# Two small tiles move from behind a kernel's weight tiles to ahead of them, which shifts these by 64 bytes

## The reference

```
h = rms_norm(x, norm_mix_pre);  z = h @ w_in              # 1024 x 2816
a = window_attention(rope(aq), rope(ak), av, sink);  r = retention(rq, rk, rv, rg, ...)
x = x + rms_norm(concat(a, r) @ w_out, norm_mix_post)
q = rms_norm(x) @ xa_wq;  kv = rms_norm(mem) @ xa_wkv     # cross-attention, 256 memory tokens
x = x + rms_norm(softmax(q k / 16) v @ xa_wo, norm_xa_post)
gate, up = split(rms_norm(x) @ ffn_w_gu);  f = (silu(gate) * up) @ ffn_w_down   # width 2816
x = x + rms_norm(f, norm_ffn_post)
```

## Time and profile before

| | |
|---|---|
| median of 3 runs | 1411.92 us (1411.61 to 1412.18) |
| span of the profiled execution, and its own time | 1411.1 us, 1411.1 us |
| TensorE (PE) busy | 1393.6 us, 6756 matmuls |
| weight loads (PEld) busy | 1154.0 us |
| VectorE, ScalarE, GpSimd busy | 858.8, 646.7, 822.7 us |
| DMA | 172.04 MB, mean 122 GB/s |
| granted TensorE clock | 1.000 |

### The profile page before, as it was taken

One profiled execution on the slowest core, in us unless ns is written; L12 is line 12 of the kernel. 1 busy time (PEld: TensorE's weight loads), 2 busy tenths in 40 slices (PEclk: granted clock), 3 DMA queues, 4 the chain that ended last, 5 costly groups with the idle time before them and its releaser, 6 DMA issues.

```text
span 1411.1 us, 18901 instructions
## 1 busy us (share of the span) xinstructions
PE 1393.6 (99%) x6756; PEld 1154.0 (82%) x6756; DVE 858.8 (61%) x1264; ACT 646.7 (46%) x1315; POOL 822.7 (58%) x574
## 2 busy tenths in 40 slices
PE   8999999999999999999999999999999999999998
PEld 7988888767988888888888888888888888878886
DVE  5699997887855767855267633333323333474868
ACT  6432233676544754354365433333333333544454
POOL 1597256103582665511354687777777774799653
PEclk9999999999999999999999999999999999999999
DMA  5676133100043464310535133333333324933353
GB/s 201 206 248 208 46 90 104 61 1 2 1 155 119 133 227 128 97 38 27 183 105 209 51 104 107 112 112 101 109 104 98 112 83 161 357 112 99 109 206 150
DMA packets 127309, 172.04 MB, mean 122 GB/s; under 512 B 9584, under 2 KB 73456, under 8 KB 127216
## 3 DMA queue, kind: packets, MB, share of 16 engines
q1 hardware_dynamic: 123776, 161.52, 34.5%
q10 hardware_dynamic: 3440, 9.32, 1.9%
HBM read 129.64 MB, written 41.16 MB: 121 GB/s over the span
## 4 chain that ended last, share of the span: by engine, by line
PE 84%; DVE 5%; POOL 4%; ACT 2%; issue 2%; DMA 2%; SPq 0%; DVEq 0%; POOLq 0%; ACTq 0%
PE ps L1167 24%; PE ps L1169 24%; PE ps L1168 24%; PE ps L1163 5%; PE ps L1598 2%; PE ps L1341 1%; PE ps L1455 1%; POOL wd L1133 1%; PE ps L1379 1%; DMA gain_b<-f_rows 1%; PE ps L1433 1%; POOL right_b L1124 1%; DVE x L3360 1%; POOL right_a L1124 1%; POOL ws L1081 1%
## 5 line engine op out<-in xcount | busy, mean ns | idle before, releaser
L1167 PE MATMUL ps<-w_hi,t_hi 128*128 128x512 f32 (+2 forms) x592 | 228.3, 386 | 1.7 <-DVE t_lo L2616 1.3
L1169 PE MATMUL ps<-w_hi,t_lo 128*128 128x512 f32 (+2 forms) x592 | 226.0, 382 | 0.0
L1168 PE MATMUL ps<-w_lo,t_hi 128*128 128x512 f32 (+2 forms) x592 | 224.4, 379 | 0.0
L962 POOL TENSOR_TENSOR w_lo<-raw,w_hi 128x512 fp32r<-128x512 f32 (+1 forms) x52 | 83.5, 1611 | 97.2 <-ACT w_hi L1877 97.0
L1167 PEld LDWEIGHTS ps<-w_hi,t_hi 128*128 128x128 f32 x592 | 112.0, 189 | 20.5 <-DVE t_lo L2616 1.9
L1169 PEld LDWEIGHTS ps<-w_hi,t_lo 128*128 128x128 f32 x592 | 111.8, 189 | 20.2
L1168 PEld LDWEIGHTS ps<-w_lo,t_hi 128*128 128x128 f32 x592 | 112.0, 189 | 19.2
L1051 POOL TENSOR_TENSOR w_lo<-raw,w_hi 128x512 fp32r<-128x512 f32 x32 | 41.9, 1316 | 99.1 <-ACT w_hi L2264 99.1
L3253 DVE TENSOR_TENSOR ev<-ps,ev 128x512 f32<-128x512 f32 x21 | 14.5, 692 | 138.6 <-PE ps L1169 138.6
L1877 ACT ACTIVATE w_hi<-raw 128x512 fp32r<-128x512 f32 (+1 forms) x52 | 31.5, 616 | 97.5 <-PE ps L1169 97.1
L2463 ACT ACTIVATE ev<-ps 128x512 f32<-128x512 f32 x63 | 37.7, 598 | 83.7 <-PE ps L1169 83.7
(11 more groups left out here) (374 smaller groups left out, 4042.3 us busy)
## 6 DMA issues: line engine op xcount, KB each, us to landing
raw_a<-in_ffn_w_gu_dram SPq DMA_DIRECT2D x44, 256.0 KB, 3.2
raw_b<-in_ffn_w_gu_dram SPq DMA_DIRECT2D x44, 256.0 KB, 3.2
f_rows<-fs SPq DMA_DIRECT2D x44, 256.0 KB, 3.7
gain_b<-f_rows SPq DMA_DIRECT2D x39, 256.0 KB, 2.8
tables<-f_rows SPq DMA_DIRECT2D x38, 256.0 KB, 2.6
f_rows<-fa SPq DMA_DIRECT2D x33, 256.0 KB, 3.4
raw<-in_xa_wkv_dram SPq DMA_DIRECT2D x32, 256.0 KB, 3.4
raw<-in_xa_wo_dram SPq DMA_DIRECT2D x32, 256.0 KB, 2.6
```

The costliest lines, as they stand in the source:

```text
L962: nc.gpsimd.tensor_tensor(w_lo[:, k, 0:width], raw[:, k, 0:width], w_hi[:, k, 0:width].bitcast(F32), ALU.subtract).then_inc(w_split, 1)
L1167: nc.tensor.matmul(out, a_hi, b_hi, start=start, stop=False, skip_group_check=onto)
L1168: nc.tensor.matmul(out, a_hi, b_lo, start=False, stop=False, skip_group_check=onto)
L1169: return nc.tensor.matmul(out, a_lo, b_hi, start=False, stop=stop, skip_group_check=onto)
```

## The change

`zero` and `eps`, tiles of one float32 for each partition, 32 bytes each with the rounding, are allocated right behind `ident` and ahead of region R; before, they stood behind `gain_b`. R, `tables`, `gain_a` and `gain_b` thereby start 64 bytes further on. `ident`, `one` and everything behind it keep their places. No instruction, semaphore or transfer is added, removed or moved.

```diff
         ident = sb("ident", [P, P])
+        zero = sb("zero", [P, 1])
+        eps = sb("eps", [P, 1])
 
         R = overlay(
...
         gain_a = sb("gain_a", [P, D])
         gain_b = sb("gain_b", [P, D])
-        zero = sb("zero", [P, 1])
-        eps = sb("eps", [P, 1])
         one = sb("one", [P, 1])
```

## The result

The changed kernel takes 1416.48 us (median of 6 runs, 1415.59 to 1417.14) beside 1412.17 us of the kernel before (6 runs, 1411.61 to 1412.55): a ratio of 1.0031, 95% interval 1.0019 to 1.0042. It is slower by 4.3 us. The forecast was 1414.2 us, in a range of 1401.5 to 1420.

The account below looks back on a forecast made before the run. TensorE's matmul spacing was taken to bound the kernel. Moving from R +3.2, 416-wide +0.4, stationary in R -1.3, switches and other engines 0, sum +2.3 us on 1411.9: 1414.2 us, range 1401.5 to 1420.

Parts of the forecast that it names:

- The bound and the place: TensorE, busy 1393.6 of 1411.1 us, bounds the kernel; the change can act only through the spacing of its matmul starts.
- d, the distance modulo 256: Moving tile's offset less the stationary tile's, modulo 256, sets matmul spacing: 226.7 ns at 0, 228.8 at 64, 233.3 at 192.
- I take the value on the line through 0, 64 and 192: Matmul spacing at the new, unmeasured distance of 128 bytes, claimed to be 231.1 ns by a straight line.
- Moving from R: 1464 512-wide matmuls with moving tile in R, stationary in H or Z: 228.9 to 231.1 ns, +3.2 us.
- Stationary in R: 588 matmuls of query projection, its sums and FFN with `wz`: 233.4 to 231.1 ns, -1.3 us.
- 416-wide: 192 matmuls 416 columns wide, each slowed by 2.2 ns: +0.4 us.
- Switches between R and Z: Slow settling after some 21 pairs of switches in the down projection: 0 us, bound -1.1 us.
- B: Rival: period 128 bytes, or 128 as good as 0, so all regions agree; 1403.3 us, -0.6%; chance 0.25.
- C: Rival: both kinds of matmul, moving or stationary in R, go to 228.9 ns; 1409.3 us; chance 0.09.
- E: Rival: no effect, spacing follows something else and the port rule holds for small shifts; 1411.9 us; chance 0.08.
- D: Rival: distance 128 conflicts as badly as 192; 1419.4 us, up to 1434.2 at the outer bound; chance 0.15.
- A: The forecast case: spacing at 128 lies in between, 230.1 to 232.0 ns; 1414.2 us, own range 1412 to 1416.3; chance 0.38.

## Why the prediction came out as it did

**The bound and the place: right.** (Of the 17 us in which PE isn't busy the prediction showed 5; another 5.4 lie behind the last matmul, which starts at 1405.28. That doesn't touch the argument.) PE set the end, no wait came or went, and the change acted through the spacing alone. That the other tiles' 64 bytes cost nothing was assumed, and the run with `tables` and the gains alone showed it (1412.31).

**d, the distance modulo 256: right.** It was read out of four stretches of one trace. The period (R 256 bytes on: 1412.5) and the independence of the place (everything 64 bytes on: 1412.49; H and Z in R's stead: 1404.32 beside 1404.12) came out. The independence of the role came out at 0, 32, 64, 192 and 224 bytes, within 0.1 ns between the input and the query projection; at 128 there are 232.4 and 233.3 ns, and as both also occur in one role, d fixes the spacing there to 1 ns and no better.

**"I take the value on the line through 0, 64 and 192": wrong.** This is the step that failed. The one-to-three ratio of 2.2 and 6.7 ns is an accident. Measured are 226.7 at 0, 228.9 at 64 and 232.4 to 234.3 at all six other multiples of 32. There is a floor at 0, a lesser one at 64, and a plateau. The line gave 231.1 ns at 128 for both kinds; it is 232.4 to 233.3 where the moving tile lies in R and 233.3, no less than before, where the stationary one does. The prediction had said that if one group changed and the other didn't, d wasn't the one cause. That sign came (+3.5 and 0.0 ns in the stretches named) and misled: it presumed that a change of d always changes the spacing, and 128 and 192 lie on one plateau.

**The terms.** Moving from R: +3.2 us forecast, +4.3 measured by the table of stages (the 96 with `z_r` belong to the input projection, not to the output one; their number stands). Stationary in R (query projection and FFN up): -1.3 forecast, +0.1 measured. 416-wide: +0.4 forecast, -0.3 measured. Their 2.3 ns over 186.7 at d = 64 were read rightly, but they are no excess over d = 0: with R 192 bytes on the same 20 intervals take 3.77 us again, 188.5 ns. This width has another curve (3.74 us at 128 and 192, 3.85 at 32, 3.86 at 96), lower at 128 and 192, where the 512-wide ones are slower. Switches between R and Z: 0 forecast, -0.3 measured over the whole down projection, and the reason was wrong. Two steps of 128 bytes were to cost as much as one of 64 and one of 192; but a pair of 24 and 24 takes 10.93 us with 64 and 192, 10.90 with 128 and 10.88 with 0. The errors, +1.1, +1.4, -0.7 and -0.3, make 1.5 of the 2.3 us between 1414.2 and 1416.5. Of the rest 0.3 us is the base (1411.9 beside 1412.2), and 0.5 is the difference between the medians and this pair of traces. So the total came near in part by errors that cancelled.

**The rivals.** B (a period of 128) and C (228.9 ns for both kinds) are out. E is out: 8 us hang on 64 bytes. By the rule weighed there (the Trainium skill, "SBUF — State Buffer", section "Who interferes with whom": PE has a read port for each operand and waits for no one), as the prediction worked it out, none of these kernels should differ from another. The measurements, 1404.1 to 1420.2 us, decide against taking it as a promise that the operands' places don't matter. Of what it says about other engines no run here is a direct test; none of PE's longest waits was for their access to a tile, and moving the tables and gains that they read cost nothing. D said that d = 128 is as bad as 192, and by the spacing this is what happened (232.4 to 233.3 and 233.3 beside 233.3, over the 231.5 from which D was to decide). Its 1419.4 was too high since it took the 416-wide ones along, with 4.5 ns each, gave 4.5 ns to all 1464 of the others, where 0 to 4.4 came, and left out the switches. A, the forecast, had the sign, but neither the spacing (230.1 to 232.0) nor, by 0.2 us, the time of its own range (1412 to 1416.3). That 1416.5 lies in the stated range of 1401.5 to 1420 is due to the width of that range, which took in D as well.

**What stays open.** Why 32 bytes are worse than 64, why d = 128 gives 232.4 ns in one stretch and 233.3 in another, why matmuls 416 wide go by another curve, and what sets the order of long and short intervals: in the input projection before, with d = 64 for every matmul, the three lines have 231.7, 226.0 and 229.0 ns. The spacings repeat exactly (25.40 to 25.41 us for the 111 intervals in the kernels with R at 0 and at 256 bytes), and one third of the matmuls out of step slows the rest, which speaks for a coupling from one matmul and weight load to the next; no run here separates the two. A tile of each operand at a free offset in a kernel without anything else would.

## What to carry to other kernels

Where TensorE is the bound and its matmuls follow each other without waits, try to lay all tiles that it reads a multiple of 256 bytes from one another. Here, for fp32r matmuls of 128x512 with a weight load each, six small tiles allocated ahead of R, or one pad of 64 bytes behind them, gave 8 us of 1412 (0.6%), while 64 bytes put ahead of R, the change, lost 4. Read the distance of two starts in the timeline for each pair of regions; two spacings for one shape are the sign. Don't draw a line through three spacings, and keep all tiles of a sequence in step: one of three out of it brought the input projection to 232.0 ns, more than the 228.9 with all of them 64 bytes out. And before two traces are compared, compare their starts: one execution's slow first microseconds were worth 1.1 us, a quarter of the effect.

## What the runs showed of the hardware

- In six of twelve traces some twelve intervals between matmuls of 352 columns near the start are 0.29 us each, and in the six others most are 0.16, as later on; the view gives a granted clock of 1.00 there in the trace before as in the trace after. What decides between them no run here shows.
- The spacing of fp32r matmuls of 128x512, each with its own weight load, ran from 226.7 to 234.3 ns at one and the same clock, by the distance of the two operands modulo 256 bytes. 32 bytes off the best place cost 6.6 ns, 64 bytes only 2.2.
- The sequence keeps a state. After a switch from tiles in Z to tiles in R, 64 bytes apart, though each pair is in step with itself, 11 intervals take 2.53 us instead of 2.49; where all are in step (R 192 bytes on), the same 11 take 2.49. Here too the distance counts: with R 128 bytes on, which exchanges 64 and 192, the blocks of 24 in R and in Z exchange their times, 5.48 and 5.45 us.
- VectorE, ScalarE, GpSimd and the DMA queues showed no effect on the time from 64 bytes on `tables` and the gains (ratio 0.9999, 0.999 to 1.0008).
